# Joint attention: norms one unit ahead, masks two units ahead, and turned keys copied in PE's order

## The reference

```
n = RMSNorm(x);  A | B both read n @ w_in
h = x + concat(A(n), B(n)) @ w_out
y = h + PEER(RMSNorm(h))
A: softmax attention, 8 heads x 64, branches (window, dilation) = (128,1), (512,4), (2048,16),
   merged with weights proportional to their softmax denominators
   prompt: over its own 512 tokens;  sample: over 2048 cached keys and values and its own 4
B: gated DeltaNet, 4 heads, key and value dim 128, chunked
PEER: 16384 single-neuron experts, product keys, top 16
```

## Time and profile before

| | |
|---|---|
| median of 3 runs | 2309.22 us (2308.1 to 2314.87) |
| the profiled execution: its time / its span | 2308.13 / 2306.3 us |
| granted TensorE clock, mean of the span | 0.947 of full |
| joint attention stage: first scores to last fold | 277.6 to 464 us |
| PE busy from 270 to 470 us | 159.9 of 200 us |
| DVE / ACT busy there | 80.0 / 67.4 of 200 us |

### The profile page before, as it was taken

How to read it: one execution, slowest core, us unless ns; L and a number is a source line. 1 busy time by engine, 2 the same in 40 slices (tenths; PEclk the granted TensorE clock), 3 DMA queues, 4 the chain that set the end, 5 groups by cost and what they waited for, 6 DMA issues and landing times.

```text
span 2306.3 us, 34698 instructions
## 1 busy us (share of the span) xinstructions
PE 2050.8 (89%) x12706; PEld 1908.5 (83%) x12706; DVE 1583.5 (69%) x3094; ACT 771.7 (33%) x1228; POOL 1159.3 (50%) x632
## 2 busy tenths in 40 slices
PE   5999878786768897999998888889989999999998
PEld 5989744575748896998888887889979999999998
DVE  2478443344433202779986999994469999999996
ACT  3223133323221323444444334333323333333332
POOL 2336000031113232477676343437788888888884
PEclk9999787988958898999999999999989999999999
DMA  5664354243523254477778567769979998999894
GB/s 183 214 224 158 133 160 160 66 164 156 190 76 122 85 230 166 145 243 225 233 236 272 214 237 263 257 239 367 364 273 315 320 318 309 309 319 313 313 325 139
DMA packets 176598, 520.95 MB, mean 226 GB/s; under 512 B 15153, under 2 KB 86065, under 8 KB 170705
## 3 DMA queue, kind: packets, MB, share of 16 engines
q1 hardware_dynamic: 136560, 290.94, 36.7%
q0 software_dynamic: 36864, 134.23, 17.5%
q10 hardware_dynamic: 3056, 94.24, 10.7%
HBM read 456.81 MB, written 128.49 MB: 254 GB/s over the span
## 4 chain that ended last, share of the span: by engine, by line
DVE 42%; PE 40%; issue 6%; POOL 4%; DMA 4%; ACT 4%; SPq 0%; ACTq 0%; DVEq 0%; PEldq 0%; POOLq 0%
DVE acc_g L1883 10%; DVE act_l L1867 9%; PE bank L2241 6%; PE bank L2242 6%; PE bank L2243 6%; DVE one L1561 6%; DVE one L1560 5%; DVE rows_g L1731 3%; POOL u_lo L1706 3%; PE twin L2241 2%; PE twin L2243 2%; PE twin L2242 2%; PE twin L492 1%; PE bank L511 1%; DMA w_raw<-wpq 1%
## 5 line engine op out<-in xcount | busy, mean ns | idle before, releaser
L1706 POOL TENSOR_TENSOR u_lo<-u_raw,u_hi 128x1024 fp32r<-128x1024 f32 x128 | 316.4, 2472 | 330.4 <-ACT u_hi L1686 329.8
L2241 PE MATMUL bank<-hn_hi,u_hi 128*128 128x416 f32 x1024 | 374.6, 366 | 33.4 <-POOL u_lo L1706 32.5
L1911 POOL TENSOR_TENSOR v_lo<-v_raw,v_hi 128x1024 fp32r<-128x1024 f32 x128 | 336.6, 2631 | 70.4 <-ACT v_hi L1836 69.2
L2242 PE MATMUL bank<-hn_lo,u_hi 128*128 128x416 f32 x1024 | 363.6, 355 | 0.0
L2243 PE MATMUL bank<-hn_hi,u_lo 128*128 128x416 f32 x1024 | 362.1, 354 | 0.0
L1883 DVE SCALAR_TENSOR_TENSOR acc_g<-rows_g,coef,acc_g 128x1024 f32<-128x1024 f32 x127 | 289.9, 2282 | 17.1 <-DMA rows_g<-ev,idx_g 16.6
L2242 PE MATMUL bank<-a_lo,v_hi 128*128 128x416 f32 x768 | 269.1, 350 | 0.0
L2241 PE MATMUL bank<-a_hi,v_hi 128*128 128x416 f32 x768 | 269.1, 350 | 0.0
L2243 PE MATMUL bank<-a_hi,v_lo 128*128 128x416 f32 x768 | 269.0, 350 | 0.0
L2241 PEld LDWEIGHTS bank<-hn_hi,u_hi 128*128 128x128 f32 x1024 | 196.0, 191 | 49.1 <-POOL u_lo L1706 46.3
L1867 DVE TENSOR_TENSOR act_l<-act_l,gin 128x416 f32<-128x416 f32 x128 | 229.2, 1791 | 0.6 <-DMA act_l<-acts_dram 0.5
(11 more groups left out here) (414 smaller groups left out, 4629.3 us busy)
## 6 DMA issues: line engine op xcount, KB each, us to landing
u_raw<-eu SPq DMA_DIRECT2D x128, 512.0 KB, 4.9
v_raw<-ev SPq DMA_DIRECT2D x128, 512.0 KB, 4.7
k_s<-kc ACTq DMA_DIRECT2D x29, 1104.0 KB
v_s<-vc ACTq DMA_DIRECT2D x29, 1104.0 KB
acts_dram<-act_c SPq DMA_DIRECT2D x128, 208.0 KB, 3.9
gates_dram<-gst ACTq DMA_DIRECT2D x8, 3328.0 KB, 12.3
gin<-gates_dram SPq DMA_DIRECT2D x32, 832.0 KB, 8.1
act_l<-acts_dram SPq DMA_DIRECT2D x64, 416.0 KB, 5.6
```

The costliest lines, as they stand in the source:

```text
L1706: nc.gpsimd.tensor_tensor(out=u_lo[s][:], in0=u_raw[2 * (x % 2) + s][:], in1=u_hi[s][:].bitcast(F32), op=ALU.subtract).then_inc(dn["ulo"], 1)
L1911: nc.gpsimd.tensor_tensor(out=v_lo[f % 4][:], in0=v_raw[f % 4][:], in1=v_hi[f % 4][:].bitcast(F32), op=ALU.subtract).then_inc(dn["vlo"], 1)
L2241: nc.tensor.matmul(out, ah, bh, start=first and i == 0, stop=False)
L2242: nc.tensor.matmul(out, ah, bl, start=False, stop=False)
```

## The change

In DVE's list the norm becomes a function, and runs one unit ahead of PE's `turn`; masks run two units ahead instead of one. The copies of turned keys stand in the unit in which PE turns them, one at its start and one at its end. In ACT's list exponentials run two units ahead, the copy of a turned unit moves into the unit itself, and the order of the copies of keys follows PE. PE's and SP's lists, buffers, shapes and the number of instructions stay.

```diff
-            mask(0)
-            for u in range(len(UNITS)):
-                b, k = divmod(u, SLOTS_B)
-                if k in (1, 2):
-                    keys(b, 2 * k - 1)
-                if u + 1 < len(UNITS):
-                    mask(u + 1)
-                if k in (0, 1):
-                    keys(b, 2 * k)
+            def norm(u):
                 n = (UNITS[u][0] + 1) * P
                 dve.wait_ge(s_exp, u + 1)
                 chain.link(nc.vector.reciprocal(smax[:, u % 4, 3:4], smax[:, u % 4, 2:3]))
                 nc.vector.tensor_scalar(sm[:, u % 4, 0:n], sm[:, u % 4, 0:n], smax[:, u % 4, 3:4], None, ALU.mult).then_inc(s_norm, 1)
+
+            mask(0)
+            mask(1)
+            norm(0)
+            for u in range(len(UNITS)):
+                b, k = divmod(u, SLOTS_B)
+                if k in (0, 1):
+                    keys(b, 2 * k)
+                if u + 1 < len(UNITS):
+                    norm(u + 1)
+                if u + 2 < len(UNITS):
+                    mask(u + 2)
+                if k in (0, 1):
+                    keys(b, 2 * k + 1)
                 if k == 1 and b:
                     sample_norm(b - 1)
                 if k == 3:
                     sample_mask(b)
                     if b:
                         own_heads(b - 1)
...
             exponentials(0)
+            exponentials(1)
             for u in range(len(UNITS)):
                 b, k = divmod(u, SLOTS_B)
-                if k in (1, 2):
-                    keys(b, 2 * k - 1)
-                if u >= 3 and u % 2:
-                    pair(u // 2 - 1)
-                if u:
-                    turned(u - 1)
                 if k == 0 and b >= 2:
                     keep_heads(b - 2)
                 if k in (0, 1):
                     keys(b, 2 * k)
-                if u + 1 < len(UNITS):
-                    exponentials(u + 1)
+                if k == 2 and b:
+                    sample_turned(b - 1)
+                if u >= 3 and u % 2:
+                    pair(u // 2 - 1)
+                turned(u)
+                if k in (0, 1):
+                    keys(b, 2 * k + 1)
+                if u + 2 < len(UNITS):
+                    exponentials(u + 2)
                 if k == 0 and b:
                     sample_exp(b - 1)
-                if k == 2 and b:
-                    sample_turned(b - 1)
-            turned(len(UNITS) - 1)
             pair(len(UNITS) // 2 - 1)
```

## The result

| | before | after |
|---|---|---|
| median, us (lowest to highest) | 2309.21 (2298.71 to 2326.14) | 2317.39 (2313.70 to 2324.74) |
| span of the profiled execution, us | 2306.3 | 2315.8 |
| granted TensorE clock, mean of the span | 0.947 | 0.943 |
| joint attention: first scores to last fold, us | 277.7 to 463.7 | 275.1 to 470.1 |

The ratio of after to before is 1.004, with a 95% interval of 1.0025 to 1.0054: 8 us slower, where 28 were forecast. The span grew by 9.5 us, and 9.0 of them are the stage's: 195.0 us where it had been 186.0. So the answer lies in this stage. By its parts: groups 0 and 1, up to the first fold, take 34.5 us where they took 37.8; groups 2 to 5 take 97.1 where they took 93.6; what follows takes 63.4 where it took 54.6.

What follows compares the result with a forecast made beforehand. PE's waits and clock in joint attention were taken to bound the kernel. From 2308.1 us, waits +0.9 (-20.7 + 5.6 + 16.0), clock -13.1 + 38 + 3, gave 2337 us; range 2308 to 2354.

Steps and rivals of the forecast that it cites:

- the norm: Joint attention: with the norm done one unit ahead, all 17 waits of PE before `turn` go, -20.7 us.
- `sample_norm`: At k = 1 it stands behind the last copy of keys, so `turn_sample` waits some 1.6 us, not 0.81: +5.6 us.
- the fold's chain: At k = 3 a mask delays `sample_mask` and `own_heads`, so PE waits at the folds opening groups 2 to 7: +16.0 us.
- the copy of the third turned pair: On ACT, behind two exponentials; hidden in groups 4 to 7, so nothing was taken, with 1 us as upper bound.
- the price of a fall: Clock falls to 1.2 GHz at the heads of groups 2 to 7: 9.5 us each, 38 for four.
- the 13.1 us of before's two falls: Clock falls in groups 3 and 5 of the kernel before, 6.5 and 6.6 us, expected to go: -13.1 us.
- the 3 us for `turn_sample`: Allowance for the new 1.6 us wait before `turn_sample` pulling the clock down in groups spared at the fold: +3 us.
- a fall now lasts until PE is in or behind `sample_scores`: Length of a fall, beginning at the head of the group, about 8 us earlier than the one in group 3.
- That the clock holds at the folds: Rival, at the six fold waits: none pulls the clock down, 2296 us, faster; chance 0.10.
- One or two falls: Rival, no change: one or two falls at the folds replace today's two, 2305 or 2315 us; chance 0.12.
- That every fold pulls the clock down: Rival, slower still: all six folds fall, 2353 us; chance 0.12 for all six and worse.
- the row: Trace of before, 414.13 to 417.83: transposes and waits alone, clock 1.00; by it transposes hold the clock, four of six stand.

Runs made afterwards that it cites:

- The two experiments that undo them: Kernel after, DVE order changed: `sample_mask` and `own_heads` ahead of the mask at k = 3, 2284.93 us; or `sample_norm` ahead of mask and keys at k = 1, 2307.14 us.
- the kernels without them: Kernel after with `sample_mask` and `own_heads` ahead of the mask, 2284.93 us; kernel after with 14 unused transposes ahead of each of six folds, 2301.96 us.
- The kernel before with the fold's wait added: Kernel before, with DVE doing the mask of unit 4b+5 ahead of `sample_mask` and `own_heads` at k = 3, norms still late: 2354.63 us, ratio 1.0212.
- `sample_norm` first: Kernel after, with DVE doing `sample_norm` at k = 1 ahead of the mask and the second copy of keys: 2307.14 us, ratio 0.9989.
- `pair` first: Kernel after, with ACT's copy of a finished pair of heads at the head of odd units, ahead of the copies of keys: 2311.61 us, ratio 1.0011.
- the runs with a fill: Kernel after with unused PE work ahead of each of six folds: 14 transposes 2301.96 us, 20 matmuls 2313.30 us, 8 matmuls 2304.17 us.

## Why the prediction was right and wrong

**Right: the norm.** All 17 waits went, -20.7 us, with nothing in their place at that spot.

**Right: the two steps that ended behind other work.** `sample_norm` was given +5.6 us and took +5.0; the fold's chain was given +16.0 and took +15.4, each wait 0.07 to 0.16 us under its sum of links. At `turn_sample` the wait is 1.53 us, where 1.6 was said. The two experiments that undo them show each by itself.

**Missed: `pair`.** The forecast priced the copy of the third turned pair on ACT and took nothing for it; PE indeed waits less for `kt_lo`, -1.6 us. But what stands behind that copy in ACT's list is `pair`, and `values` two units on waits for its bank: +4.7 us. Its links were in the earlier trace rows and were not followed to the next waiter. With it the waits sum to -20.7 + 5.0 + 15.4 + 4.7 - 1.6 = +2.8 us, where +0.9 was forecast.

**Wrong: the price of a fall.** The step that failed is "So 6.5 + 4 - 1 = 9.5 us each, 38 for four". More folds pulled the clock down than forecast (six of six), but one costs 3.2 to 3.4 us by the stage of the kernels without them. Six falls cost some 20 us; with the 13.1 us of before's two falls taken off, the clock is left with some 6 to 7, where the forecast had -13.1 + 38 + 3 = +27.9. The stage agrees: 195.0 - 186.0 = 9.0 us longer, less 2.8 of waits, leaves 6.2 for the clock. What the 3 us for `turn_sample` stood for happened once in after, in group 7, from 449.8 to 453.1 us.

The reason stands in the words "a fall now lasts until PE is in or behind `sample_scores`". The forecast let each fall last some 20 us; they lasted 7.2 on average. The length was read from a kernel in which PE stood 1.18 to 1.31 us for the norm, twice in the same group, while the clock was low. The change takes just those waits away, so behind the fold PE is busy almost without a gap (3.20 of 3.20 us in the shortest stretches), and the clock comes back sooner. The kernel before with the fold's wait added is the test: the same waits at the folds, the norm waits kept, and more than twice the time at 1.2 GHz.

Within one kernel the moment of the fall goes with its length. In the traces of after and of the runs with `sample_norm` first and `pair` first, the clock falls at 17 folds. The seven falls that come 0.7 to 1.6 us before PE starts the fold, while it still waits, last 10.0 to 13.5 us; the ten that come behind its start last 3.2 to 6.7. In the kernel before with the fold's wait, four falls come behind the start of the fold, and with the norm's waits there they last 9.5 to 23.5: longer than any of those ten, which bears the account out; the two that come in the wait last 9.9 and 30.3. That the fall's moment causes its length is not shown, and what sets the moment is open: no run here varied it.

**The rivals.** That the clock holds at the folds is refuted by the windows. One or two falls, "the same", gave 2305 or 2315 us. The time came just above that, but by six cheap falls and not by two dear ones, so the nearness is chance. That every fold pulls the clock down is what happened; its 2353 us fell with the price. That the time lies between 2308 and 2354 us and the change is slower, as forecast, is in part luck too: the count of falls was too low and the price of one about three times too high.

**The rule on transposes.** The Trainium skill, "TensorE: Matmul & The Clock Gate", Part 4 (PE-mode transpose), says that transposes do not count as PE's activity for the full clock as other matmuls do. The runs with a fill say otherwise for these f32 transposes, 2301.96 us against 2304.17 with matmuls and 2317.39 with none; the measurement decides. The forecast's choice of the row over the rule stands, though it was no reason to take four falls and not six.

## What to carry to other kernels

When a step is moved earlier in an in-order list, ask of every instruction behind it who waits for it next: a mask that was not needed for another unit held two steps whose inputs were ready, and with them PE for 15.4 us. Price a fall of the clock by the work that stands behind it in the new kernel, not by the falls of the old one: here the change closed the gaps there, and the clock came back sooner. And when a change is a trade of short waits for long ones, undo its side effects one at a time: the norms one unit ahead are 8 us slower than before as they were put in, and 34 us faster with three steps moved into the order in which PE asks for them.

## What the runs showed of the hardware

- Fourteen f32 transposes of 128 x 128 (1.75 us) in a wait of 2.5 us kept the granted clock at 1.00 in all six groups, and eight plain matmuls (2.05 us) did the same; without either it fell to 0.50 in all six.
- The same wait of 2.45 us was followed by 10.0 us at 1.2 GHz in one kernel and by 23.5 us in another, where PE had three more waits of 0.81 to 1.18 us in that stretch.
- Of 24 waits of 2.36 to 2.72 us at a fold, in four traces, 23 were met by a fall to 1.2 GHz; at one of 2.72 us the clock stayed at 1.00.
- A plain f32 matmul of 128 x 128 stands twice in the timeline: 20 of them are x40 and take 4.73 us, 0.12 us each entry; a transpose stands once, 14 of them in 1.75 us, 0.125 us each.
